# An encoder layer on one core: the experts' second product from split operands, and one room fewer for their first weights

## What is computed

```
def expert_block(args):
    xblk, e = args
    gt, up = jnp.split(xblk @ w13[e], 2, axis=-1)      # 128 x 1024 @ 1024 x 512
    return (jax.nn.silu(gt) * up) @ w2[e]              # 128 x 256  @ 256 x 1024
...
yb = lax.map(expert_block, (xb, blk_e)).reshape(P, D)
out = jax.ops.segment_sum(yb.astype(jnp.float32) * buf_w[:, None], buf_tok, num_segments=N + 1)[:N]
...
x = x + gate2 * hier_moe(h2, w_rg, b_rg, w_re, b_re, w13, w2)
```

## Time and profile before

| | us |
|---|---|
| median of 3 runs (lowest and highest) | 2607.66 (2596.43 to 2608.02) |
| the profiled execution | 2606.3 |
| its span in the profile | 2604.5 |
| PE busy | 2375.6 (91%) |
| DVE, ACT, POOL busy | 1653.5, 1124.3, 796.3 |
| mean granted clock of PE, full speed being 1 | 0.964 |
| the blocks 4 to 33, of which the change speaks, in the span | 2259 to 2583 |

### The profile page before, as it was taken

How to read it: one execution, slowest core, us unless ns; L and a number is a source line. 1 busy time by engine, 2 the same in 40 slices (tenths; PEclk the granted TensorE clock), 3 DMA queues, 4 the chain that set the end, 5 groups by cost and what they waited for, 6 DMA issues and landing times. The chain is left out here.

```text
span 2604.5 us, 53583 instructions
## 1 busy us (share of the span) xinstructions
PE 2375.6 (91%) x22387; PEld 1890.6 (73%) x22387; DVE 1653.5 (63%) x2459; ACT 1124.3 (43%) x1945; POOL 796.3 (31%) x511
## 2 busy tenths in 40 slices
PE   4999999999997989899889799998998996989997
PEld 2778777788886888888778666666877884556664
DVE  4744468966563455455467566766986886666664
ACT  3310033344341566666455455553122221666664
POOL 2122144544443434554113200001300000445554
PEclk7999999999998999899989999999999997999998
DMA  7233434443434233232144611104756446899994
GB/s 305 95 134 138 144 108 146 145 153 133 150 120 168 60 96 98 61 98 77 39 136 118 156 39 31 31 13 146 245 161 228 156 146 230 317 336 352 328 307 110
DMA packets 196194, 394.07 MB, mean 151 GB/s; under 512 B 39857, under 2 KB 105169, under 8 KB 182897
## 3 DMA queue, kind: packets, MB, share of 16 engines
q1 hardware_dynamic: 173776, 322.58, 37.0%
q0 software_dynamic: 12960, 36.59, 5.0%
q10 hardware_dynamic: 9216, 31.46, 3.0%
HBM read 294.57 MB, written 106.48 MB: 154 GB/s over the span
## 5 line engine op out<-in xcount | busy, mean ns | idle before, releaser
L99 PE MATMUL ps_in<-h_t_low,w_in_high 128*128 128x512 f32 x960 | 381.2, 397 | 0.0
L100 PE MATMUL ps_in<-h_t_high,w_in_low 128*128 128x512 f32 x960 | 374.2, 390 | 0.0
L101 PE MATMUL ps_in<-h_t_high,w_in_high 128*128 128x512 f32 x960 | 373.9, 390 | 0.0
L99 PEld LDWEIGHTS ps_in<-h_t_low,w_in_high 128*128 128x128 f32 x960 | 180.2, 188 | 47.7 <-issue 9.3
L1271 POOL TENSOR_TENSOR wkv_levels<-wkv_nt,level_mask 128x1024 f32<-128x1024 f32 x60 | 140.5, 2362 | 233.9 <-ACT wkv_nt L1216 233.9
L101 PEld LDWEIGHTS ps_in<-h_t_high,w_in_high 128*128 128x128 f32 x960 | 180.2, 188 | 38.1
L100 PEld LDWEIGHTS ps_in<-h_t_high,w_in_low 128*128 128x128 f32 x960 | 180.4, 188 | 34.9
L508 ACT COPY p_row<-ps_in 128x512 f32<-128x512 f32 x72 | 42.0, 588 | 288.3 <-PE ps_in L101 244.6
L330 POOL CAST w_in_high<-w_in_tile 128x1024 fp32r<-128x1024 f32 x40 | 47.8, 1195 | 341.9 <-PE ps_in L101 341.0
L3077 PE MATMUL ps_xy<-w_tile,hidden_turned 128*128 128x512 f32 x272 | 126.5, 609 | 12.4 <-DMA w_tile<-in_w 11.0
L2226 POOL TENSOR_TENSOR fin_y<-fin_y 128x1024 f32<-128x1024 f32 x6 | 16.3, 2714 | 365.0 <-DMA fin_y<-wkv_y 365.0
(11 more groups left out here) (432 smaller groups left out, 6296.8 us busy)
## 6 DMA issues: line engine op xcount, KB each, us to landing
merged_t<-in_w SPq DMA_DIRECT2D x36, 1024.0 KB, 11.2
w_tile<-in_w SPq DMA_DIRECT2D x34, 1024.0 KB, 15.0
w_now<-in_w SPq DMA_DIRECT2D x30, 1024.0 KB, 13.7
wkv_in<-front_area SPq DMA_DIRECT2D x24, 1024.0 KB, 5.0
w_in_tile<-in_w_in SPq DMA_DIRECT2D x40, 512.0 KB, 3.6
front_area<-in_w_ada SPq DMA_DIRECT2D x8, 2048.0 KB, 9.4
p_t<-p_mixed ACTq DMA_DIRECT2D x24, 512.0 KB, 3.2
gates<-p_mixed ACTq DMA_DIRECT2D x16, 768.0 KB, 4.0
```

The lines of the kernel that those rows point to most:

```text
L99: nc.tensor.matmul(out, w[0], x[1], start=start, stop=False)
L100: nc.tensor.matmul(out, w[1], x[0], start=False, stop=False)
L101: return nc.tensor.matmul(out, w[0], x[0], start=False, stop=stop)
```

## The change

- The hidden rows of a block from t = 4 on (FIRST_SPLIT_OUT) are kept by ACT as a high part `hid_hi` in place of the plain copy, and DVE makes their low part `hid_lo` (`hidden_low`).
- ACT casts w2 of the block to its high part (`out_weights_high`, 128x2048); it waits for the load of w2 and for the second product of the block before, since the high part has one buffer. The low part is made in two halves, one by POOL and one by DVE (both called `out_weights_low`, 128x1024 each).
- PE makes the second product with `split_product`: 12 matmuls of 128x512 in place of 8, and waits for the low parts.
- On ACT, `keep_turned` and `out_weights_high` now stand ahead of `weigh_gates`. On POOL, the low half stands ahead of `gate_rows`. On DVE, `hidden_low` and the low half stand at the end of the step.
- MORE goes from 3 to 2, so SLOTS from 6 to 5: `w13_now` has two rooms.

```diff
-        MORE = 3
+        MORE = 2
...
+            def out_weights_low(t, b):
+                pool.wait_ge(m["w2_hi"], t - FIRST_SPLIT_OUT + 1)
+                nc.gpsimd.tensor_tensor(w2_lo[:, 0], w2[:, b, 0], w2_hi[:, 0].bitcast(F32), ALU.subtract).then_inc(m["w2_lo"], 1)
...
+                if 3 <= t < STATIC + 3 and split_out(t - 3):
+                    out_weights_low(t - 3, (t - 3) % 2)
                 if 3 <= t < STATIC + 3:
                     gate_rows(t - 3, (t - 3) % 2)
...
+                if split_out(t):
+                    pe.wait_ge(m["hid_lo"], t - FIRST_SPLIT_OUT + 1)
+                    pe.wait_ge(m["w2_lo"], 2 * (t - FIRST_SPLIT_OUT) + 2)
...
-                        mm = nc.tensor.matmul(ps_xy[b][:, c], hid_t[:, b, k], w2[:, b, k, 512 * c:512 * c + 512], start=(k == 0), stop=(k == F2 - 1))
+                        if split_out(t):
+                            mm = split_product(nc, ps_xy[b][:, c], (hid_hi[:, b, k], hid_lo[:, b, k]), (w2_hi[:, k, at], w2_lo[:, k, at]),
+                                               start=(k == 0), stop=(k == F2 - 1))
...
-                nc.scalar.copy(hid_t[:, b], ps_ht[:]).then_inc(m["hid_t"], 1)
+                nc.scalar.copy((hid_hi if split_out(t) else hid_t)[:, b], ps_ht[:]).then_inc(m["hid_t"], 1)
+
+            def out_weights_high(t, b):
+                act.wait_ge(w2_in[b], turn_no(t, b))
+                act.wait_ge(m["y_full"], t)
+                nc.scalar.copy(w2_hi[:], w2[:, b]).then_inc(m["w2_hi"], 1)
...
+                keep_turned(t, b)
+                if split_out(t):
+                    out_weights_high(t, b)
                 weigh_gates(t, b)
-                keep_turned(t, b)
...
+            def hidden_low(t, b):
+                dve.wait_ge(m["hid_t"], t + 1)
+                V.tensor_tensor(hid_lo[:, b], ps_ht[:], hid_hi[:, b].bitcast(F32), ALU.subtract).then_inc(m["hid_lo"], 1)
+
+            def out_weights_low(t, b):
+                dve.wait_ge(m["w2_hi"], t - FIRST_SPLIT_OUT + 1)
+                V.tensor_tensor(w2_lo[:, 1], w2[:, b, 1], w2_hi[:, 1].bitcast(F32), ALU.subtract).then_inc(m["w2_lo"], 1)
...
                 if t >= 1:
                     keep_output(t - 1, 1 - b)
+                if split_out(t):
+                    hidden_low(t, b)
+                    out_weights_low(t, b)
```

More of the change, by code:

```diff
@@ L2822, in route_and_experts @@
         hid = s.sb("hidden", [P, D_EXPERT])
-        hid_t = s.sb("hidden_turned", [P, 2, F2, P])
+        with ExitStack() as plain_hidden:
+            hid_t = plain_hidden.enter_context(nc.sbuf_tensor("hidden_turned", [P, 2, F2, P], F32))
+        hid_hi = s.sb("hidden_high", [P, 2, F2, P], F32R)
         yb = s.sb("yb_tile", [P, 2, D])
@@ L2851, in route_and_experts @@
         xt_hi, xt_lo = ([s.sb(f"xb_{n}{b}", [P, DF, P], F32R) for b in range(2)] for n in ("high", "low"))
+        hid_lo = s.sb("hidden_low", [P, 2, F2, P], F32R)
+        w2_hi, w2_lo = (s.sb(f"w2_{n}", [P, F2, D], F32R) for n in ("high", "low"))
         w_hi, w_lo = s.sb("w13_high", [P, DF, 2 * D_EXPERT], F32R), s.sb("w13_low", [P, DF, 2 * D_EXPERT], F32R)
         m = {n: s.sem("moe_" + n) for n in ("own", "g_exp", "ratio", "hot_rows", "ids_full", "ids", "blocks", "routed",
-                                            "unread", "cleared", "turned", "x_hi", "x_lo", "w_hi", "w_lo", "h_half", "h_full", "tanh", "gated", "hidden", "ht_full", "hid_t",
+                                            "unread", "cleared", "turned", "x_hi", "x_lo", "w_hi", "w_lo", "w2_hi", "w2_lo", "hid_lo", "h_half", "h_full", "tanh", "gated", "hidden", "ht_full", "hid_t",
                                             "y_full", "y_kept", "gates_in", "row_weights", "part_weighed", "weighed", "row_gated")}
@@ L2861, in route_and_experts @@
         FIRST_SPLIT = 3
+        FIRST_SPLIT_OUT = 4
         ks = lambda h: slice(HK * h, HK * h + HK)
@@ L2886, in halves, with split_out @@
             return t + (h + 1 + 2 * (STATIC - FIRST_SPLIT) - (OWN + 3))
+        def split_out(t):
+            return isinstance(t, int) and t >= FIRST_SPLIT_OUT
         def over_pairs(eng, body):
@@ L3065, in turn_hidden @@
                     pe.wait_ge(m["hid_t"], t)
+                if isinstance(t, int) and split_out(t - 1):
+                    pe.wait_ge(m["hid_lo"], t - FIRST_SPLIT_OUT)
                 for k in range(F2):
@@ L3074, in out_of_hidden @@
                 pe.wait_ge(m["x_lo"], t + x_turned)
+                if split_out(t):
+                    pe.wait_ge(m["hid_lo"], t - FIRST_SPLIT_OUT + 1)
+                    pe.wait_ge(m["w2_lo"], 2 * (t - FIRST_SPLIT_OUT) + 2)
                 for c in range(2):
+                    at = slice(512 * c, 512 * c + 512)
                     for k in range(F2):
-                        mm = nc.tensor.matmul(ps_xy[b][:, c], hid_t[:, b, k], w2[:, b, k, 512 * c:512 * c + 512], start=(k == 0), stop=(k == F2 - 1))
+                        if split_out(t):
+                            mm = split_product(nc, ps_xy[b][:, c], (hid_hi[:, b, k], hid_lo[:, b, k]), (w2_hi[:, k, at], w2_lo[:, k, at]),
+                                               start=(k == 0), stop=(k == F2 - 1))
+                        else:
+                            mm = nc.tensor.matmul(ps_xy[b][:, c], hid_t[:, b, k], w2[:, b, k, at], start=(k == 0), stop=(k == F2 - 1))
                 mm.then_inc(m["y_full"], 1)
```

## The result

The changed kernel takes 2671.4 us in the median of 6 runs (2654.07 to 2686.16), the kernel before 2607.8 (2596.43 to 2614.91). The ratio is 1.0249, with a 95% interval of 1.0219 to 1.0279: 2.5% slower, where 0.6% was forecast. The profiled execution of the changed kernel took 2670.1 us, its span is 2668.2, 63.7 longer than the span before. The direction was right. The size was not: +17 was forecast, and the range ended at 2642.

What follows compares the result with a forecast made beforehand. It took DMA (11.16 us a block plus loss, 11.76) to bound blocks 4 to 29 and an ACT-DVE loop of 10.61 the tail; +9.7, +1.8, -0.5 and +6.0 gave +17.0 on 2606.3, so 2623 us, range 2602 to 2642.

Steps and rivals of the forecast that it cites:

- the other DVE work: DVE's hidden low part and half of w2's fit its 2.47 us wait: no cost; without cover 1.6 us a block.
- The step on POOL: POOL's half of w2's low part: 2.72 us, hidden with 1.4 to spare; contended 3.80, total 1.1 more at the end.
- rival 3: The clock falls after PE's waits between products: +20 or +10 us on top, so 2633; chance 0.06.
- PE will be idle about 2.4 us in each 11.8: PE's idle time per block, from which the clock's fall was sized, taken as in every fourth block.
- Blocks 4 to 29: 25 x 11.76: Stretch with busy DMA: 11.76 us a block, 294.0 for 284.3, +9.7 us.
- Three blocks at 10.61: Blocks after the last w13 loads: 10.61 us each for 10.01, +1.8 us.
- Last block and end: Last block 8.66 us for 9.14, -0.5; the end behind it +6.0 us.
- The loop of 10.6: ACT, DVE and PE from one turned hidden block to the next: 10.61 us, longer than PE's 9.34.
- 8 to 12 forecast: w2's landing after issue over blocks 4 to 29: 8 to 12 us, where it was 15.1 in the median.
- The room: Third room for first weights given up: no block waits for w13, but 2.1 MB more while DMA is busy, 6.1 us.
- The end: After the last turn: last scatter 12.6 us later, 4.73 behind the scatter before it, +6.0 in all.
- both loops: ACT and DVE's loop within one block, 10.61 us, and w2's latency loop over two blocks, (L+12.64)/2 a block.

Runs made afterwards that it cites:

- e2: Changed kernel with the whole low part of w2 made by DVE in one 128x2048 instruction, none by POOL: 2638.7 us.
- e6: Changed kernel with four spare 128x439 matmuls ahead of PE's wait in odd blocks, their output unread: 2661.4 us, ratio 1.0196.
- e3: As e2, with ACT's row weights again ahead of the hidden rows' copy and w2's cast: 2620.4 us.
- e1: Kernel before with two rooms instead of three for first weights (MORE 2), nothing else: 2604.7 us.
- e9: As e3, with w2's cast and low part moved into the next step, behind those of the rows: 2618.4 us, ratio 1.0034.
- e4: Changed kernel with only ACT's old order put back (row weights first), POOL keeping its half of w2: 2652.3 us.
- e5: Changed kernel with the whole low part of w2 made by POOL (128x2048), none by DVE: 2669.3 us.
- e7: Kernel before with MORE 2 and one spare POOL sum of two SBUF tensors per block, timed to meet DVE's w13 subtraction: 2611.9 us, ratio 1.0009.
- e8: As e7, but the spare POOL instruction is a copy with one SBUF input: 2610.1 us, ratio 1.0009.
- e11: Kernel before with w2's load issued ahead of the step's w13 halves, nothing else: 2604.5 us, ratio 0.9990.
- e10: As e9, with w2's load issued ahead of the step's w13 halves: 2617.2 us, ratio 1.0045.

## Why the prediction was wrong

**The step that failed** is the one on the other DVE work: "The other DVE work [...] fits where DVE now waits 2.47 for the cast of w13; it costs nothing". Half of w2's low part was taken as half of 2.29 us. It took 1.23 only where DVE came first; the mean was 3.19 and the worst 5.40, more than the 2.47 of cover. The step on POOL named a price of contention on POOL's side alone, 3.80 for 2.72, and +1.1 us in all. POOL's side was cheap, 2.43 in the median and hidden inside the stage. The price was on DVE's side, on the loop, and the half of w2 on POOL held up DVE's subtractions of w13 as well. e2 prices it: without POOL's half, 30 of the 65 us (2.49% of 2608) are gone, give or take 13, clock falls that followed from it among them. That is most, not all, of the 47 us by which the forecast missed: e2 is still 35 us slower than the kernel before, where 17 were forecast for the change. Its blocks 4 to 29 take 12.29, not 11.76, and nothing here divides that difference.

The prediction cited the Trainium skill (GPSIMD Engine Reference, Specifications) for the shared interfaces. The Trainium skill says more on another page (SBUF — State Buffer, Summary: rules for kernel authors): when VectorE's instruction has two SBUF inputs and GpSimd's reads SBUF, the second one to issue blocks fully until the first has finished. The rows above agree with that: 3.23 for 2.29 on DVE behind one instruction of POOL, and 3.44 for 2.41 on POOL behind one of DVE. That DVE mostly waits for two of POOL's (5.40) is a thing that only the rows show. A rival of this kind was missing from the prediction: POOL's row weights of 2.35 and its half of w2, about as long, stand back to back; met by a DVE instruction of 1.2 they are up to +4.7 on DVE. Less the 2.47 of cover that leaves over 2 us in a block that meets both. Measured were +4.2 on the instruction and 2.5 on the block.

**The clock** (rival 3, given 0.06) did fall. The step that mis-sized it is "PE will be idle about 2.4 us in each 11.8": idle time was 3.64 in one wait, in every long block, and the fall cost 2.6 us each time. e6 puts it at 14 of the 65 us, give or take 13, with the fewer meetings of DVE and POOL in that run in it. Its chance of 0.06 was too low, since the wait that brought it was not among those priced.

**What else was mis-sized.** "Blocks 4 to 29: 25 x 11.76" measured 13.40: +41 us. "Three blocks at 10.61" measured 12.92: +6.9. Last block and end together were 0.6 below the forecast, and block 4 was reached 0.7 us earlier. These add up to the 47 us between 2623.3 and 2670.1.

**What was right.** The loop of 10.6: the short block is 10.6 and the 0.9 of DVE's stretch, e2's last blocks are 10.6 and a stretch of 0.47, and taking the row weights out of it (e3) gave 0.7%. The low parts were not late inside the stage, only at the end, as forecast. w2 lands in 9.9 us (8 to 12 forecast), though at 13.4 a block and not at 11.8. The room costs nothing (e1). The end came out near the forecast, 13.3 us from the end of the last turn to the last scatter for 12.6, and +4.8 in all for +6.0, but not by the path that was summed: the last scatter waited for DVE's weighing of PE's last product, and not 4.73 us behind the scatter before it. That product began 6.2 us after the turn, when POOL's half was done, and ran at the lower clock, 12 matmuls in 5.3 us. That the two paths are about equally long is luck. And e9, the change without POOL's half and with both loops opened, runs at 11.76 a block and 2618 us: about the forecast, in a kernel where the excluded step does not occur. That the figures coincide to the hundredth is chance, since its loops are different ones.

**What stays open.** Of the 65 us the steps e2 (30), e3 (18) and e9 (8, not clear of noise by itself) take back 56, each measured behind the one before. The last 9 lie in the end and in blocks 4 to 29: in e9's profiled execution 27.35 us pass behind the last turn, for 21.70, and these blocks take 11.76 for 11.37. What part w2's latency has in them was not separated. That the alternation of short and long blocks feeds itself, a slow product letting DVE catch up and come first, is read from the timelines and was not tested. Nor is it known what lets a waiting DVE instruction in between two of POOL's: it happened in 28 of 69 such meetings over the changed kernel, e4, e5, e6 and e7, and in none of e5's ten.

## What to carry to other kernels

Two engines that share a resource are not two engines. Before half of a VectorE instruction with two SBUF inputs is given to GpSimd, lay both timelines over each other and ask who starts first; if GpSimd does, add what is left of its instruction to VectorE's path, and as the upper bound the whole of what it runs back to back. The sharing cost more here than doing all of it on VectorE (e2 is 1.15% faster). And before PE is relieved, add up the instructions of the engine that feeds it: DVE's came to 10.00 us a block, and PE's old pace was 10.01.

## What the runs showed that I had not expected

- A waiting DVE instruction often does not get in between two POOL instructions: 5.40 us for 1.2 beside 2.41 and 2.39 (13 of 16 times in the changed kernel), and 5.56 for 2.29 in e7 (three of seven times there).
- Once it may go, it takes its full time: in every meeting where POOL's instruction had begun first and had over 0.1 us to go, DVE's 128x2048 ended 2.15 us and its 128x1024 1.09 us behind the end of the last POOL instruction it had waited for.
- A POOL copy with a single SBUF input, 1.03 us, excludes DVE's subtraction as well: 3.08 for 2.29 in e8.
- A kernel can carry this unseen. e7's subtractions of w13 reached 7.1 us, and its time was that of the kernel before within 0.3%. The two of 7.1 even began 0.24 us ahead of POOL's sum, but while POOL's gather was being issued; what held them at that moment the trace does not say.
- The order in which w2 and w13 are issued to one queue changed w2's landing by little, and not for the better: 15.1 and 15.8 us in the kernel before and e11, 13.1 and 14.4 in e9 and e10 (medians over 2250 to 2640 us).
